# Local attention scores as three split products, their low parts made on VectorE

## The chip, the cores and the metric

The kernel runs on one core of one Trainium2 chip. The metric is the device time of one execution in microseconds. The engines are TensorE (PE), VectorE (DVE), ScalarE (ACT), GpSimd (POOL) and SyncE (SP), each with its own instruction stream, coupled by semaphores.

## The reference

Two layers over x (512 tokens, 1024 channels). Each layer forms u = RMSNorm(x), one combined input projection, three branches (a gated short convolution, gated linear attention, local attention), a gated sum of the branches, the output projection, and then an MLP. The change lies in the local attention: 8 query heads, 2 key heads, 64 channels a head, blocks of 128 queries against their own and the previous block of 128 keys.

```python
q = rms_norm(q.reshape(Bsz, S, SWA_HEADS, SWA_HEAD_DIM).astype(f32), qn_w)
k = rms_norm(k.reshape(Bsz, S, SWA_KV_HEADS, SWA_HEAD_DIM).astype(f32), kn_w)
q = rope_partial(q, cos, sin) * SWA_HEAD_DIM ** -0.5
k = rope_partial(k, cos, sin)
s = jnp.einsum('bnqkgd,bnckd->bkgnqc', qb, kw)
s = jnp.where(mask, s, -jnp.inf)
m = jnp.maximum(jnp.max(s, axis=-1, keepdims=True), sink)
p = jnp.exp(s - m)
denom = jnp.sum(p, axis=-1, keepdims=True) + jnp.exp(sink - m)
o = jnp.einsum('bkgnqc,bnckd->bkgnqd', p, vw) / denom
```

## The kernel before

All large products are split products. A float32 matrix is held as a high part of type float32r and a low part (value minus high part), and PE adds three products: high by high, high by low, low by high. ACT makes the high part of each weight unit, DVE the low part (L1229, `split_low`), and PE waits for `lo_done` of the unit. The small products of the branches, the attention scores among them, are plain float32.

Every engine runs down a list of words written out by hand: PE_ORDER, ACT_ORDER, DVE_ORDER for the projection and branch stage. A word with a plus is a weight split (`+gr2` is the split of the weight unit gr2); the others are steps. `gr0.0` on PE is one token tile of a projection unit. The words that matter here, in the stage of local attention:

- KD and QT0 to QT3: PE transposes the key and four pairs of query heads into a PSUM bank (L738). ACT copies the bank to SBUF (L1027, tiles `swa_k` and `swa_q`), frees the bank and adds one to `qT_ready`.
- ATT0, ATT1: products and masking of the linear attention (PE L754, DVE L1471).
- SC0 to SC7: the scores, on PE L810, in banks a and b for even and odd heads. SC0 to SC3 are the four query blocks of the first half of the heads, SC4 to SC7 those of the second. SC0 and SC4 have 128 keys, the others 256. SC waits for `qT_ready` of its half. On DVE the step SC masks the scores and takes the row maxima (L1520 to L1534); on ACT it is the exponential.
- SM: DVE forms the reciprocal sum (L1538, L1540), ACT scales the probabilities.
- PT: PE transposes the probabilities (L820), DVE copies them under a mask to `probs_keys` (L1546) and adds one to `probs_T_ready`.
- PV: PE multiplies the probabilities with the values (L828), after `probs_T_ready`.
- KV0, KV1: states of the linear attention (PE L767, DVE L1477 and L1482).

The four banks go round: a step may fill a bank when the step four fills before it has been read. QT2 takes the bank of QT0, SC0 the banks of ATT1, QT3 that of QT1, KV0 those of SC0b and QT3.

The score call of one pair of heads and one row half is

```python
last = nc.tensor.matmul(
    both[odd][:, j * 2 * P + first:(j + 1) * 2 * P],
    sq[r:r + SWA_DIM, 2 * half + j, n * P:(n + 1) * P],
    kd[r:r + SWA_DIM, (n - 1) * P + first:(n + 1) * P], start=True, stop=True)
```

with j and odd from 0 to 1, so four calls a block and 64 in the program.

Of the kernel before, what the change touches and what calls it, by code (L numbers as in the profile page):

```python
# [9 lines left out]
D_MODEL, SEQ, DEPTH = 1024, 512, 2  # L10
P = 128
# [3 lines left out]
SWA_HEADS, SWA_KV, SWA_DIM = 8, 2, 64  # L15
# [5 lines left out]
             sq=512, sk=128, sv=128, gates=N_BRANCH * D_MODEL)  # L21
# [72 lines left out]


DVE_ORDER = """+gk1 UT0 UT1 UT2 UT3 RN +kva0 NROW gk0 +kva1 +kva2 gk1 +kva3 +sq0 +sq1 kva0 kva1 kva2 kva3 +sq2 AT +sq3 +gv0 ZA ZB
sq0 sq1 sq2 sq3 +gv1 +gv2 X0 +gv3 QS +gr0 QM +gr1 X1 QR ATT0 +gr2 ATT1 +gr3 SC0 +cx0 SM0 SC1 KV0 SM1 PT0 +cx1 KV1 PV0 PT1 +cx2
gr0 SC2 gr1 gr2 SC3 gr3 +cx3 SM2 GO0 SM3 cx0 GO1 OS PT2 YG0 cx1 YG1 +cc0 +cc1 cx2 +cc2 PV1 PV2 cx3 +cc3 PT3 SC4 cc0 ct0 SM4
SC5 +cb0 YT0 +cb1 cc1 PV3 SM5 cc2 +cb2 YT1 PT4 cc3 SC6 +cb3 YT2 PV4 SM6 cv0 PT5 +gate0 YT3 ct1 SC7 cl0 ct2 SM7 PT6 PV5 cv1 cv2
+gate1 +gate2 cl1 PT7 ct3 +gate3 PV6 cv3 cl2 +br0 cl3 gate0 PV7 gate1 +br1 gate2 +br2 gate3""".split()  # L100
# [133 lines left out]
def hybrid_trunk(nc, x, x_cols, positions, params, w_in, gla_wa2, w_branch, w_o, w_up, w_down, norms, consts, gmask, out):  # L234
    f32, f32r, i32 = mybir.dt.float32, mybir.dt.float32r, mybir.dt.int32
    ALU, ACT, AX = mybir.AluOpType, mybir.ActivationFunctionType, mybir.AxisListType
    ctx = ExitStack()
    with ctx:
# [3 lines left out]
        def at(name, tile, shape, dt=f32, extra=0):  # L242
            return nc.alloc_sbuf_tensor_at(name, [P] + shape, dt, offset=BASE + tile * TILE + extra)
# [43 lines left out]
        attm = at("gla_att", 76, [GLA_HEADS, TT, P])  # L287
        sm = [at(f"probs{i}", 80 + 2 * i, [4, P]) for i in range(2)]
        gt = at("gate_tanh", 80, [4, SEQ])
        sq = at("swa_q", 84, [4, SEQ])  # L290
        kd = at("swa_k", 88, [SEQ])
        vd = at("swa_v", 90, [TT, SWA_KV, SWA_DIM])
        pT = at("probs_keys", 91, [2, 4, P])
        th = [at(f"gla_gate_tanh{i}", (93, 98)[i], [SEQ]) for i in range(2)]
# [68 lines left out]
        def sem(name):  # L363
# [21 lines left out]
         conv_val, conv_hi, yconv_ready, pv_hi, yswa_ready, scores_ready, exps_ready, den_ready,  # L385
         probs_ready, probs_T_ready, gate_scaled, gate_ready, mixed_done, mx_hi, mx_ready, x_upd,
         x_summed, u_hi, u_ready, hid_val, hid_hi, hid_ready, sums_val, sums_hi, sums_ready, diff_val, diff_hi,
         diff_ready, ws_val, ws_hi, ws_ready, wg_ready, g_full, x_left_added, x_right_added, folded, fold_scaled, x_top_folded, x_low_folded, x_first_added, angle_ready, sines_ready, first_full, first_hi, first_lo, probs_T_zero) = map(sem, """
         par_free hi_done lo_done unit_done tile_done bank_full ready0 rs_ready a_ready ga_ready
         z_biased softplus_ready b_ready gla_exps gla_qk kva_read sq_sq sq_summed v_ready gr_tanh rg_ready  # L390
         kendT_ready att_ready states_ready yo_sq yo_summed ytok_ready gla_hi ygla_ready q_roped qT_ready
         conv_val conv_hi yconv_ready pv_hi yswa_ready scores_ready exps_ready den_ready
         probs_ready probs_T_ready gate_scaled gate_ready mixed_done mx_hi mx_ready x_upd
         x_summed u_hi u_ready hid_val hid_hi hid_ready sums_val sums_hi sums_ready diff_val diff_hi
         diff_ready ws_val ws_hi ws_ready wg_ready g_full x_left_added x_right_added folded fold_scaled x_top_folded x_low_folded x_first_added angle_ready sines_ready first_full first_hi first_lo probs_T_zero""".split())

        UNIT_CREDIT = SPLIT

# [176 lines left out]
        def _(pe):  # L575
# [127 lines left out]
            for l in range(DEPTH):  # L703
                for step in PE_ORDER if l else PE_FIRST + PE_ORDER[PE_ORDER.index("kva0"):]:
                    word, pieces = pieces_of(step)
                    kind, i = step_of(word)
# [66 lines left out]
                    elif kind == "GO":  # L773
                        both = [open_bank(l, word + half) for half in "ab"]
                        pe.wait_ge(att_ready, l * 4 + 4)
                        pe.wait_ge(states_ready, l * 2 + 2)
                        for t in (2 * i, 2 * i + 1):
                            for pair in range(2):
                                at_o = slice((t % 2 * 2 + pair) * P, (t % 2 * 2 + pair + 1) * P)
                                for odd in range(2):  # L780
                                    h = 2 * pair + odd
                                    nc.tensor.matmul(both[odd][:, at_o], attm[:, h, t, :], vt[:, t, h * P:(h + 1) * P],  # L782
                                                     start=t % 2 + pair == 0, stop=False)
                        for c in range(4 * i, 4 * i + 4):
                            to = slice(GLA_CHUNK * (c % 2), GLA_CHUNK * (c % 2 + 1))
                            for pair in range(2 if c else 0):
                                at_o = slice((c // 2 % 2 * 2 + pair) * P, (c // 2 % 2 * 2 + pair + 1) * P)
                                for odd in range(2):
                                    r = GLA_DK * odd
                                    last = nc.tensor.matmul(both[odd][to, at_o],  # L790
                                                            gq[r:r + GLA_DK, pair, c * GLA_CHUNK:(c + 1) * GLA_CHUNK],
                                                            S[r:r + GLA_DK, pair, c - 1, :], start=False,
                                                            stop=c % 4 >= 2 and pair == 1)
                                    if c % 4 == 3 and pair == 1:
                                        last.then_inc(bank_full, 1)
                    elif kind == "YT":
                        b = open_bank(l, word)
                        pe.wait_ge(ytok_ready, l * 2 + 2)
                        for t in range(TT):
                            last = nc.tensor.transpose(b[:, t * P:(t + 1) * P], yo[t // 2][:, t % 2, i, :], ident)  # L800
                        last.then_inc(bank_full, 1)
                    elif kind == "SC":
                        half, n = i // TT, i % TT
                        pe.wait_ge(qT_ready, l * 5 + 3 + 2 * half)
                        both = [open_bank(l, word + part) for part in "ab"]
                        first = 0 if n else P
                        for j in range(2):
                            for odd in range(2):
                                r = SWA_DIM * odd
                                last = nc.tensor.matmul(  # L810
                                    both[odd][:, j * 2 * P + first:(j + 1) * 2 * P],
                                    sq[r:r + SWA_DIM, 2 * half + j, n * P:(n + 1) * P],
                                    kd[r:r + SWA_DIM, (n - 1) * P + first:(n + 1) * P], start=True, stop=True)
                                if j == 1:
                                    last.then_inc(bank_full, 1)
                    elif kind == "PT":
                        pe.wait_ge(probs_ready, l * 8 + i + 1)
                        b = open_bank(l, word)
                        for h in range(4):
                            last = nc.tensor.transpose(b[:, h * P:(h + 1) * P], sm[i % 2][:, h, :], ident)  # L820
                        last.then_inc(bank_full, 1)
                    elif kind == "PV":
                        half, n = i // TT, i % TT
                        b = open_bank(l, word)

                        def weighted(kv, cur):
                            r = SWA_DIM * kv
                            return nc.tensor.matmul(b[r:r + SWA_DIM, 2 * kv * P:(2 * kv + 2) * P], vd[:, n - 1 + cur, kv, :],  # L828
                                                    pT[:, cur, 2 * kv:2 * kv + 2, :].rearrange("p h c -> p (h c)"),
                                                    start=cur == 0 or n == 0, stop=cur == 1)  # L830
                        pe.wait_ge(probs_T_ready, l * 8 + i + 1)
                        if n:
                            for kv in range(SWA_KV):
                                weighted(kv, 0)
                        for kv in range(SWA_KV):
                            last = weighted(kv, 1)
                        last.then_inc(bank_full, 1)
# [36 lines left out]
        def _(act):  # L874
# [6 lines left out]
            def filled(l, name):  # L881

                f = FILL[l, name]
                act.wait_ge(bank_full, f + 1)
                return bank[f % 4], bank_free[f % 4]
# [68 lines left out]
            for l in range(DEPTH):  # L954
                for word in ACT_ORDER:
# [67 lines left out]
                        nc.scalar.activation(kendT[:, i].rearrange("p t n -> p (t n)"), b[:], ACT.Copy).then_inc(free, 1)  # L1023
                        nc.scalar.drain().then_inc(kendT_ready, 1)
                    elif kind in ("KD", "QT"):
                        b, free = filled(l, word)
                        nc.scalar.activation(kd[:] if kind == "KD" else sq[:, i, :], b[:], ACT.Copy).then_inc(free, 1)  # L1027
                        nc.scalar.drain().then_inc(qT_ready, 1)
                    elif kind == "GO":
                        if i:  # L1030
                            act.wait_ge(yo_summed, l * 4 + 2)
# [177 lines left out]
        def _(dve):  # L1209
# [8 lines left out]
            def filled(l, name):  # L1218

                f = FILL[l, name]  # L1220
                dve.wait_ge(bank_full, f + 1)
                return bank[f % 4], bank_free[f % 4]
# [107 lines left out]
            for l in range(DEPTH):  # L1330
                for word in DVE_ORDER if l else DVE_FIRST + DVE_ORDER[DVE_ORDER.index("+kva3") + 1:]:
# [173 lines left out]
                    elif kind == "YT":  # L1505
# [2 lines left out]
                        V.scalar_tensor_tensor(out=yl[:, 4 + i, :], in0=b[:], scalar=par[:, PC["on"]:PC["on"] + 1],  # L1508
                                               in1=yh[:, 4 + i, :].bitcast(f32), op0=ALU.mult, op1=ALU.subtract).then_inc(free, 1)
                        V.drain().then_inc(ygla_ready, 1)  # L1510
                    elif kind == "SC":
                        buf = i % 2
                        if i >= 2:
# [297 lines left out]
```

## Time and profile before

| | before |
|---|---|
| median of 3 runs | 1562.13 us (1561.9 to 1562.47) |
| the profiled execution | 1561.48 us |
| its span, first to last instruction | 1559.7 us |
| PE busy | 1548.6 us (99%) |
| DVE busy | 1051.2 us (67%) |
| ACT busy | 753.5 us (48%) |
| POOL busy | 113.0 us (7%) |
| granted TensorE clock over the span | 1.000 |

The span is one execution taken by the profiler. Busy is the time in which an engine ran at least one instruction. The recorded matmuls of PE overlap, since they are pipelined, so the distance between their starts tells their cost, not their duration. A row of a timeline puts like instructions together; a count behind x is their number, and its start is that of the first one.

### The profile page before, as it was taken

The numbers are of one execution on the slowest core, as the hardware profiler recorded it, in microseconds if no ns is written. First come the engines' busy times: TensorE is split into PE (matmuls) and PEld (weight loads), VectorE is DVE, ScalarE is ACT, GpSimd is POOL, SyncE is SP. The second block draws the span as 40 slices with busy tenths as digits, with TensorE's granted clock in tenths as the row PEclk, the third lists the DMA queues.
The fourth block names the chain that finished last, engine by engine and source line by source line (L and its number), as shares of the span: only waits on it lengthen the run. The fifth ranks groups of instructions, "written<-read, shape, count | busy, mean of one in ns | idle before, by whom it ended". The sixth has DMA issues, their size and how long they took to land.

```text
span 1559.7 us, 21296 instructions
## 1 busy us (share of the span) xinstructions
PE 1548.6 (99%) x7440; PEld 1266.4 (81%) x7440; DVE 1051.2 (67%) x1529; ACT 753.5 (48%) x1147; POOL 113.0 (7%) x97
## 2 busy tenths in 40 slices
PE   8999999999999999999999999999999999999999
PEld 7877778888878888888888777788888788888887
DVE  5677774555777657586857787755457676665778
ACT  5656532223556463546546465332236564636363
POOL 0000000000211010111200000000002111101011
PEclk9999999999999999999999999999999999999999
DMA  6321314532686655647533212155317856666555
GB/s 228 116 83 57 107 54 149 176 114 75 133 213 160 181 133 151 170 109 206 89 101 102 82 55 82 55 175 176 108 54 149 242 122 186 139 174 137 137 133 122
DMA packets 133722, 204.16 MB, mean 131 GB/s; under 512 B 6704, under 2 KB 83056, under 8 KB 133616
## 3 DMA queue, kind: packets, MB, share of 16 engines
q1 hardware_dynamic: 107600, 153.30, 29.5%
q0 software_dynamic: 25296, 48.76, 18.7%
q8 instruction: 60, 0.98, 0.3%
q10 hardware_dynamic: 720, 0.74, 0.1%
q14 instruction: 46, 0.38, 0.1%
HBM read 170.80 MB, written 2.10 MB: 111 GB/s over the span
## 4 chain that ended last, share of the span: by engine, by line
PE 87%; DVE 8%; issue 2%; DVEq 1%; DMA 1%; ACT 1%; ACTq 0%; POOL 0%; POOLq 0%
PE acc L609 19%; PE acc L611 19%; PE acc L610 19%; PE acc L672 5%; PE acc L673 5%; PE acc L674 5%; DVE wl_rows L1229 3%; PE acc L631 3%; PE acc L633 3%; PE acc L632 3%; PE bank L810 1%; PE bank L828 1%; DMA x_tokens<-product_sums 0%; DVE mixed_s_lo L1580 0%; PE bank L782 0%
## 5 line engine op out<-in xcount | busy, mean ns | idle before, releaser
L609 PE MATMUL acc<-uh,wh 128*128 128x512 f32 x1152 | 452.9, 393 | 2.6 <-DVEq L1250 2.5
L611 PE MATMUL acc<-uh,wl 128*128 128x512 f32 x1152 | 448.6, 389 | 0.0
L610 PE MATMUL acc<-ul,wh 128*128 128x512 f32 x1152 | 448.5, 389 | 0.0
L609 PEld LDWEIGHTS acc<-uh,wh 128*128 128x128 f32 x1152 | 216.3, 188 | 54.8 <-issue 5.0
L611 PEld LDWEIGHTS acc<-uh,wl 128*128 128x128 f32 x1152 | 216.3, 188 | 45.4
L610 PEld LDWEIGHTS acc<-ul,wh 128*128 128x128 f32 x1152 | 216.4, 188 | 43.5
L1229 DVE TENSOR_TENSOR wl<-raw,wh 128x1024 fp32r<-128x1024 f32 x142 | 174.0, 1225 | 103.4 <-ACT wh L903 91.2
L903 ACT ACTIVATE wh<-raw 128x1024 fp32r<-128x1024 f32 x142 | 150.6, 1061 | 138.6 <-PE acc L611 86.3
L903 ACT ACTIVATE wh_rows<-raw_down 128x1024 fp32r<-128x1024 f32 x136 | 144.3, 1061 | 109.7 <-PE acc L674 89.0
L1229 DVE TENSOR_TENSOR wl_rows<-raw_down,wh_rows 128x1024 fp32r<-128x1024 f32 x136 | 166.6, 1225 | 23.1 <-ACT wh_rows L903 11.2
L1073 ACT ACTIVATE gate_tanh<-gate_tanh 128x512 f32<-128x512 f32 x40 | 25.3, 633 | 164.4 <-DVEq L1260 164.4
L1259 DVE TENSOR_TENSOR gate_tanh<-acc,rsqrt_rows 128x512 f32<-128x512 f32 x48 | 33.2, 691 | 97.6 <-PE acc L611 96.5
L1122 ACT ACTIVATE hidden<-acc 128x512 f32<-128x512 f32 x64 | 38.3, 599 | 122.1 <-PE acc L611 120.3
L631 PE MATMUL acc<-wh_rows,uh 128*128 128x512 f32 (+1 forms) x256 | 95.9, 375 | 0.0
L633 PE MATMUL acc<-wl_rows,uh 128*128 128x512 f32 (+1 forms) x256 | 93.4, 365 | 0.0
L632 PE MATMUL acc<-wh_rows,ul 128*128 128x512 f32 (+1 forms) x256 | 93.3, 364 | 0.0
L1159 POOL DMA_DIRECT2D raw_down<-raw_down x20 | 24.2, 1209 | 809.1 <-DMA raw_down<-in_w_o_dram 568.9
L672 PE MATMUL acc<-wh_rows,hidden_hi 128*128 128x512 f32 x192 | 75.1, 391 | 0.0
L609 PE MATMUL acc<-yh,wh 128*128 128x512 f32 x192 | 74.8, 389 | 0.0
L674 PE MATMUL acc<-wl_rows,hidden_hi 128*128 128x512 f32 x192 | 74.7, 389 | 0.0
L673 PE MATMUL acc<-wh_rows,hidden_lo 128*128 128x512 f32 x192 | 74.7, 389 | 0.0
L611 PE MATMUL acc<-yh,wl 128*128 128x512 f32 x192 | 74.7, 389 | 0.0
(268 smaller groups left out, 2435.1 us busy)
## 6 DMA issues: line engine op xcount, KB each, us to landing
raw<-in_w_in_dram SPq DMA_DIRECT2D x39, 1024.0 KB, 5.2
raw<-in_w_up_dram SPq DMA_DIRECT2D x32, 1024.0 KB, 5.9
raw_down<-in_w_down_dram SPq DMA_DIRECT2D x32, 1024.0 KB, 8.9
raw_down<-raw_down POOLq DMA_DIRECT2D x44, 512.0 KB, 5.1
raw_down<-in_w_down_dram POOLq DMA_DIRECT2D x32, 512.0 KB, 6.2
raw_branch<-in_w_in_dram SPq DMA_DIRECT2D x12, 1024.0 KB, 5.0
raw_branch<-in_w_branch_dram SPq DMA_DIRECT2D x12, 1024.0 KB, 5.1
raw_down<-in_w_o_dram SPq DMA_DIRECT2D x8, 1024.0 KB, 8.4
```

The source lines that it names most:

```text
L609: nc.tensor.matmul(a[:], wh[slot][:, k, :], right_h, start=at_k == 0, stop=False)
L610: nc.tensor.matmul(a[:], wh[slot][:, k, :], right_l, start=False, stop=False)
L611: last = nc.tensor.matmul(a[:], wl[slot][:, k, :], right_h, start=False, stop=at_k == n - 1)
L631: nc.tensor.matmul(to, left_h[:, k, s], h[:, row, 0:cols], start=k == 0, stop=False)
L632: nc.tensor.matmul(to, left_l[:, k, s], h[:, row, 0:cols], start=False, stop=False)
L633: last = nc.tensor.matmul(to, left_h[:, k, s], lo[:, row, 0:cols], start=False, stop=k == KT - 1)
L672: nc.tensor.matmul(to[:], left[0], h[:, row, :], start=k == 0, stop=False)
L673: nc.tensor.matmul(to[:], left[1], h[:, row, :], start=False, stop=False)
L674: last = nc.tensor.matmul(to[:], left[0], lo[:, row, :], start=False, stop=k == BK - 1)
L903: nc.scalar.activation(split_view(True, u, l), raw_view(u), ACT.Copy).then_inc(hi_done, 1)
L1122: nc.scalar.activation(hid[:, k, :], a[:], ACT.Relu).then_inc(free, 1)
L1229: V.tensor_tensor(split_view(False, u, l), raw_view(u), split_view(True, u, l).bitcast(f32), ALU.subtract).then_inc(lo_done, 1)
```

## The change

ACT writes the copies of key and queries as float32r (`k_hi`, `q_hi`) and no longer frees the bank. DVE gets the steps KD and QT0 to QT3: it waits for ACT's copy (`qT_hi`), subtracts it from the bank, writes `k_lo` or `q_lo`, frees the bank and adds one to `qT_ready`. PE makes each score as three products into the same bank region, so a block has 12 calls in place of 4. In DVE_ORDER the splits gr2, gr3, cx0 and cx1 change places with other steps. Apart from rounding the result is the same.

```diff
 DVE_ORDER
-sq0 sq1 sq2 sq3 +gv1 +gv2 X0 +gv3 QS +gr0 QM +gr1 X1 QR ATT0 +gr2 ATT1 +gr3 SC0 +cx0 SM0 SC1 KV0 SM1 PT0 +cx1 KV1 PV0 PT1 +cx2
+sq0 sq1 sq2 sq3 +gv1 +gv2 X0 +gv3 QS +gr0 QM +gr1 X1 QR ATT0 KD QT0 ATT1 QT1 QT2 +gr2 SC0 QT3 +gr3 SM0 SC1 KV0 SM1 +cx0 PT0 KV1 PV0 +cx1 PT1 +cx2
...
-        sq = at("swa_q", 84, [4, SEQ])
-        kd = at("swa_k", 88, [SEQ])
+        q_hi = at("swa_q_hi", 84, [4, SEQ], f32r)
+        q_lo = [at(f"swa_q_lo{i}", (100, 101, 81, 83)[i], [SEQ], f32r) for i in range(4)]
+        k_hi, k_lo = at("swa_k_hi", 88, [SEQ], f32r), at("swa_k_lo", 89, [SEQ], f32r)
...
                         for j in range(2):
-                            for odd in range(2):
-                                r = SWA_DIM * odd
-                                last = nc.tensor.matmul(
-                                    both[odd][:, j * 2 * P + first:(j + 1) * 2 * P],
-                                    sq[r:r + SWA_DIM, 2 * half + j, n * P:(n + 1) * P],
-                                    kd[r:r + SWA_DIM, (n - 1) * P + first:(n + 1) * P], start=True, stop=True)
-                                if j == 1:
-                                    last.then_inc(bank_full, 1)
+                            for term, (q, k) in enumerate(((q_hi[:, 2 * half + j], k_hi), (q_hi[:, 2 * half + j], k_lo),
+                                                           (q_lo[2 * half + j], k_hi))):
+                                for odd in range(2):
+                                    r = slice(SWA_DIM * odd, SWA_DIM * (odd + 1))
+                                    last = nc.tensor.matmul(both[odd][:, j * 2 * P + first:(j + 1) * 2 * P], q[r, queries],
+                                                            k[r, keys], start=term == 0, stop=term == 2)
+                                    if j == 1 and term == 2:
+                                        last.then_inc(bank_full, 1)
...
                     elif kind in ("KD", "QT"):
-                        b, free = filled(l, word)
-                        nc.scalar.activation(kd[:] if kind == "KD" else sq[:, i, :], b[:], ACT.Copy).then_inc(free, 1)
-                        nc.scalar.drain().then_inc(qT_ready, 1)
+                        b, _ = filled(l, word)
+                        nc.scalar.activation(k_hi[:] if kind == "KD" else q_hi[:, i, :], b[:], ACT.Copy).then_inc(qT_hi, 1)
...
+                    elif kind in ("KD", "QT"):
+                        b, free = filled(l, word)
+                        dve.wait_ge(qT_hi, l * 5 + (1 if kind == "KD" else i + 2))
+                        low, high = (k_lo[:], k_hi[:]) if kind == "KD" else (q_lo[i][:], q_hi[:, i, :])
+                        V.tensor_tensor(low, b[:], high.bitcast(f32), ALU.subtract).then_inc(free, 1)
+                        V.drain().then_inc(qT_ready, 1)
```

On DVE, from the mask copy of ATT0 to the start of SC0, there stood before (`wl_rows` with a number is the low part of a weight unit, gr2 and gr3 here; `gla_att` is ATT):

```order
L1471 COPY_PREDICATED gla_att<-masks,bank 128x512 x2
L1229 TENSOR_TENSOR wl_rows_72<-raw_branch_55,wh_rows_68 128x1024
L1471 COPY_PREDICATED gla_att<-masks,bank 128x512 x2
L1229 TENSOR_TENSOR wl_rows_73<-raw_branch_55,wh_rows_69 128x1024
L1525 TENSOR_TENSOR probs_103<-bank,consts 128x256 x2
```

and stands now, on to the split of gr3:

```order
L1472 COPY_PREDICATED gla_att<-masks,bank 128x512 x2
L1516 TENSOR_TENSOR swa_k_lo<-bank,swa_k_hi 128x512
L1516 TENSOR_TENSOR swa_q_lo_107<-bank,swa_q_hi 128x512
L1472 COPY_PREDICATED gla_att<-masks,bank 128x512 x2
L1516 TENSOR_TENSOR swa_q_lo_108<-bank,swa_q_hi 128x512
L1516 TENSOR_TENSOR swa_q_lo_109<-bank,swa_q_hi 128x512
L1230 TENSOR_TENSOR wl_rows_72<-raw_branch_55,wh_rows_68 128x1024
L1532 TENSOR_TENSOR probs_103<-bank,consts 128x256 x2
...
L1516 TENSOR_TENSOR swa_q_lo_110<-bank,swa_q_hi 128x512
L1230 TENSOR_TENSOR wl_rows_73<-raw_branch_55,wh_rows_69 128x1024
```

Two low parts stand ahead of ATT1's mask copy, two behind it, and one behind SC0; the split of gr2 moved behind four of them, that of gr3 behind SC0.

On DVE, between SM1 (the last `small` rows) and PT1, the order was before (`wl_63` is the low part of cx1, `probs_keys` is PT, `yl` is PV):

```order
L1540 RECIPROCAL small<-small 128x4
L1546 COPY_PREDICATED probs_keys<-masks,bank 128x512
L1229 TENSOR_TENSOR wl_63<-raw_52,wh_59 128x1024
L1477 COPY gla_states<-bank 128x128
L1482 SCALAR_TENSOR_TENSOR gla_states<-gla_states,gla_exp_b,bank 128x128 x6
L1557 TENSOR_TENSOR yl<-bank,yh 64x2x128 x2
L1546 COPY_PREDICATED probs_keys<-masks,bank 128x512 x2
```

and is now (`wl_62` is the low part of cx0):

```order
L1547 RECIPROCAL small<-small 128x4
L1230 TENSOR_TENSOR wl_62<-raw_52,wh_58 128x1024
L1553 COPY_PREDICATED probs_keys<-masks,bank 128x512
L1478 COPY gla_states<-bank 128x128
L1483 SCALAR_TENSOR_TENSOR gla_states<-gla_states,gla_exp_b,bank 128x128 x6
L1564 TENSOR_TENSOR yl<-bank,yh 64x2x128 x2
L1230 TENSOR_TENSOR wl_63<-raw_52,wh_59 128x1024
L1553 COPY_PREDICATED probs_keys<-masks,bank 128x512 x2
```

The split of cx0, which stood behind SC0, is now directly ahead of PT0, and that of cx1 moved from behind PT0 to behind PV0.

On PE the block SC0 was one row of four calls:

```order
L632 MATMUL acc<-wh_rows_66,ul 128x512
L633 MATMUL acc<-wl_rows_70,uh 128x512
L810 MATMUL bank<-swa_k,swa_q 128x128 x4
L738 MATMUL bank<-consts,swa_qk_tokens 128x128 x4
L631 MATMUL acc<-wh_rows_66,uh 128x512
```

and is now:

```order
L634 MATMUL acc<-wl_rows_70,uh 128x512
L814 MATMUL bank<-swa_k_hi,swa_q_hi 128x128 x2
L814 MATMUL bank<-swa_k_lo,swa_q_hi 128x128 x2
L814 MATMUL bank<-swa_k_hi,swa_q_lo_107 128x128 x2
L814 MATMUL bank<-swa_k_hi,swa_q_hi 128x128 x2
L814 MATMUL bank<-swa_k_lo,swa_q_hi 128x128 x2
L814 MATMUL bank<-swa_k_hi,swa_q_lo_108 128x128 x2
L739 MATMUL bank<-consts,swa_qk_tokens 128x128 x4
```

Its neighbours are the same, and the place of every score block in PE's list is unchanged.

## Rows read from the trace of the kernel before

**Rows 1.** The page, busy time, share of the span and instructions of TensorE.

```profile
PE 1548.6 (99%) x7440; PEld 1266.4 (81%) x7440; DVE 1051.2 (67%) x1529; ACT 753.5 (48%) x1147; POOL 113.0 (7%) x97
```

**Rows 2.** Waits of TensorE in the whole span: total, times, longest.

```profile
PE acc L609 <- DVEq L1250: 2.5, 1, 2.5
...
PE bank L689 <- DVEq L1634: 0.2, 1, 0.2
```

**Rows 3.** Line L810: durations in ns, first and last start, shapes.

```profile
L810 PE MATMUL bank<-swa_k,swa_q x128: 272/376/480, 99.9 to 970.6; 64*128 64x256 f32 x96, 64*128 64x128 f32 x32
```

**Rows 4.** The chain, TensorE, 94 to 125 us: start, length, piece.

```profile
99.92 0.65 PE bank L810 x8
...
105.28 1.06 PE bank L810 x8
```

**Rows 5.** The timeline, TensorE, inside two score blocks: start, duration, instructions.

```profile
105.53 0.60 PE L810 MATMUL bank<-swa_k,swa_q 64*128 64x256 f32 x4
...
105.75 0.60 PE L810 MATMUL bank<-swa_k,swa_q 64*128 64x256 f32 x4
...
100.07 0.50 PE L810 MATMUL bank<-swa_k,swa_q 64*128 64x128 f32 x6
...
100.18 0.39 PE L810 MATMUL bank<-swa_k,swa_q 64*128 64x128 f32 x4
```

**Rows 6.** The timeline, TensorE, split products with 272 columns.

```profile
44.01 0.29 PE L633 MATMUL acc<-wl_rows,uh 128*128 128x272 f32 x1
44.14 0.29 PE L631 MATMUL acc<-wh_rows,uh 128*128 128x272 f32 x1
```

**Rows 7.** The timeline, VectorE, 93 to 114 us, idle before in brackets.

```profile
93.10 1.61 DVE L1471 COPY_PREDICATED gla_att<-masks,bank 128x512 f32<-128x512 int32 x2 [0.23 <-issue]
94.90 1.23 DVE L1229 TENSOR_TENSOR wl_rows<-raw_branch,wh_rows 128x1024 fp32r<-128x1024 f32 x1 [0.19 <-issue]
96.23 1.61 DVE L1471 COPY_PREDICATED gla_att<-masks,bank 128x512 f32<-128x512 int32 x2
...
100.60 0.75 DVE L1525 TENSOR_TENSOR probs<-bank,consts 128x256 f32<-128x256 f32 x2 [1.35 <-PE bank L810]
...
102.53 0.15 DVE L1534 TENSOR_TENSOR small<-params,small 128x4 f32<-128x4 f32 x1
...
105.56 0.16 DVE L1538 TENSOR_TENSOR small<-small 128x4 f32<-128x4 f32 x1 [0.60 <-ACT small L1047]
...
106.38 0.42 DVE L1520 COPY probs<-bank 128x256 f32<-128x256 f32 x1 [0.40 <-PE bank L810]
...
113.55 0.74 DVE L1546 COPY_PREDICATED probs_keys<-masks,bank 128x512 f32<-128x512 int32 x1 [0.23 <-issue]
```

**Rows 8.** The page, the multiplication by a row out of an accumulator.

```profile
L1259 DVE TENSOR_TENSOR gate_tanh<-acc,rsqrt_rows 128x512 f32<-128x512 f32 x48 | 33.2, 691 | 97.6 <-PE acc L611 96.5
```

**Rows 9.** The timeline, ScalarE, 96 to 119 us.

```profile
96.50 0.60 ACT L1027 ACTIVATE swa_q<-bank 128x512 f32<-128x512 f32 x1 [0.15 <-issue]
...
105.34 0.19 ACT L1047 ACTIVATE small<-small 128x4 f32<-128x4 f32 x1
...
118.20 1.06 ACT L903 ACTIVATE wh<-raw 128x1024 fp32r<-128x1024 f32 x1 [2.26 <-PE acc L633]
```

**Rows 10.** The timeline, TensorE, 99 to 115 us.

```profile
99.86 0.71 PE L810 MATMUL bank<-swa_k,swa_q 64*128 64x128 f32 x8
...
113.43 1.09 PE L767 MATMUL bank<-gla_v_tokens,gla_k_end_tokens 64*64 64x128 f32 x28
114.48 0.65 PE L828 MATMUL bank<-probs_keys,swa_v 128*64 128x256 f32 x4
```

**Rows 11.** The chain, TensorE, second layer, 870 to 892 us.

```profile
874.37 0.65 PE bank L810 x8
...
888.97 0.62 PE bank L828 x4
```

**Rows 12.** The page, DMA issues: count, size, median us to landing.

```profile
raw<-in_w_in_dram SPq DMA_DIRECT2D x39, 1024.0 KB, 5.2
```

More of the change, by code:

```diff
@@ L387, in hybrid_trunk @@
          x_summed, u_hi, u_ready, hid_val, hid_hi, hid_ready, sums_val, sums_hi, sums_ready, diff_val, diff_hi,
-         diff_ready, ws_val, ws_hi, ws_ready, wg_ready, g_full, x_left_added, x_right_added, folded, fold_scaled, x_top_folded, x_low_folded, x_first_added, angle_ready, sines_ready, first_full, first_hi, first_lo, probs_T_zero) = map(sem, """
+         diff_ready, ws_val, ws_hi, ws_ready, wg_ready, g_full, x_left_added, x_right_added, folded, fold_scaled, x_top_folded, x_low_folded, x_first_added, angle_ready, sines_ready, first_full, first_hi, first_lo, probs_T_zero, qT_hi) = map(sem, """
          par_free hi_done lo_done unit_done tile_done bank_full ready0 rs_ready a_ready ga_ready
@@ L394, in hybrid_trunk @@
          x_summed u_hi u_ready hid_val hid_hi hid_ready sums_val sums_hi sums_ready diff_val diff_hi
-         diff_ready ws_val ws_hi ws_ready wg_ready g_full x_left_added x_right_added folded fold_scaled x_top_folded x_low_folded x_first_added angle_ready sines_ready first_full first_hi first_lo probs_T_zero""".split())
+         diff_ready ws_val ws_hi ws_ready wg_ready g_full x_left_added x_right_added folded fold_scaled x_top_folded x_low_folded x_first_added angle_ready sines_ready first_full first_hi first_lo probs_T_zero qT_hi""".split())
         UNIT_CREDIT = SPLIT
@@ L806, in _ @@
                         first = 0 if n else P
+                        queries, keys = slice(n * P, (n + 1) * P), slice((n - 1) * P + first, (n + 1) * P)
                         for j in range(2):
-                            for odd in range(2):
-                                r = SWA_DIM * odd
-                                last = nc.tensor.matmul(
-                                    both[odd][:, j * 2 * P + first:(j + 1) * 2 * P],
-                                    sq[r:r + SWA_DIM, 2 * half + j, n * P:(n + 1) * P],
-                                    kd[r:r + SWA_DIM, (n - 1) * P + first:(n + 1) * P], start=True, stop=True)
-                                if j == 1:
-                                    last.then_inc(bank_full, 1)
+                            for term, (q, k) in enumerate(((q_hi[:, 2 * half + j], k_hi), (q_hi[:, 2 * half + j], k_lo),
[6 more added lines that the diff above has]
+                                        last.then_inc(bank_full, 1)
                     elif kind == "PT":
```

## Prediction

> **What bounds the kernel now.** I read the page's busy times first. TensorE (PE) is busy for 99% of the span [rows 1], so the question is whether the change shortens PE's work or makes PE wait. The waits of PE came next: in the whole execution it has six, the longest 2.5 us, and none is at a score block or at a product of probabilities and values [rows 2]. PE runs as one unbroken chain, and a microsecond added to it or taken from it anywhere is a microsecond of the result. Then I read the changed line, L810, by shape: 128 recorded matmuls, two for each of the 64 calls, so a float32 product runs as two passes [rows 3]. 96 of them have 256 moving columns, 32 have 128. Per layer there are eight score blocks: six wide (SC1 to SC3 and SC5 to SC7), two narrow (SC0 and SC4). Last I followed DVE and ACT from the first score block to PV0, because the change puts DVE between ACT and PE there.
>
> **The score blocks on PE.** The chain gives 1.06 us to a wide block and 0.65 to a narrow one [rows 4]. Inside a block the odd and even heads use different row halves and start together, in pairs; the starts of neighbouring pairs (105.53 and 105.75 in the wide block, 100.07 and 100.18 in the narrow one [rows 5]) are about 0.215 and 0.11 us apart. Four pair steps leave a fixed part of 1.06 - 4 x 0.215 = 0.20 us, and 0.65 - 0.44 = 0.21 in the narrow block, for the change of tile shape before and behind.
>
> After the change a block has six pair steps of one pass each, two head pairs times three terms. No row shows such a step. The nearest is a split product with 272 columns, which starts every 0.125 us [rows 6]; the lower bound is the narrow step of today, 0.11, which has the same 128 columns to load. I take 0.12. A wide block becomes 6 x 0.12 + 0.20 = 0.92 us, a gain of 0.14 (0.20 at a step of 0.11, 0.11 at 0.125). A narrow block is bounded by its load and becomes 6 x 0.11 + 0.21 = 0.87, a loss of 0.22. Could a split product with few columns be slower? If its step cost what both float32 passes of a pair cost, 0.22, a narrow block would be 1.5 us, a loss of 0.9. I take 0.11 and keep that end. If only this counted, the kernel would change by -12 x 0.14 + 4 x 0.22 = -0.8 us.
>
> **The wait at SC0.** SC0 now needs the low parts of key, QT0 and QT1, all from DVE. DVE's ATT0 starts at 93.10, takes 1.61 and ends at 94.71 [rows 7]. For a low part (128x512 out of PSUM) I use the 0.691 us of L1259 [rows 8], with 0.18 between steps, the gap in front of the weight split at 94.90. The low part of the key is then done at 95.6. QT0's needs its high part, and ACT starts that at 96.50 and takes 0.60 [rows 9]: DVE idles until 97.16 and is done at 97.85. ATT1, which started at 96.23, starts at 98.03 and ends at 99.64. QT1's low part ends at 100.51. From DVE to PE I take 0.19: PT0's copy starts at 113.55, ends at 114.29, and PV0 starts at 114.48 [rows 7, 10]. SC0 starts at 100.70 in place of 99.86 [rows 10]: PE waits 0.84 us.
>
> **The wait at PV0.** This is the larger one. PV0 needs PT0's copy, and 114.48 is where PE arrives anyway: KV1 starts at 113.43 and occupies PE for 1.02 to 1.09. So there is no slack in front of PV0. DVE from 100.51 on:
>
> QT2 low 0.87; the gr2 split 1.42 (1.23 and a gap); SC0, from 100.60 to the end of its last operation (102.53 + 0.15), with a gap 2.2; QT3 low 0.87; the gr3 split 1.42; SM0 0.6; a gap of 0.2 [rows 7]. That is 7.6 us, and SC1 starts at 108.1 in place of 106.38. ACT's exponentials for SM0 do not decide it: today they end (105.34 + 0.19 [rows 9]) 2.85 us after SC0 on DVE, with a weight split ahead of them, so at the latest at 105.0 + 2.85 = 107.9, 0.4 behind where I put SM0. From SC1's start to PT0's start DVE works through 7.17 us without waiting for anyone (106.38 to 113.55), and cx0's split now stands inside that stretch, another 1.3 to 1.4. PT0 starts at 116.6, ends at 117.3, and PE starts PV0 at 117.5: 3.0 us late. On its own, PE would be late by 0.84 + 0.22 (SC0) - 0.14 (SC1) = 0.9. The other 2.1 are a wait at PV0, and up to there the length of the PE blocks no longer matters; even the dear narrow block (0.9) is absorbed.
>
> As a cross-check: five low parts with gaps are 4.35 us of new DVE work and the idling for QT0 is 1.6, together 5.9; DVE's idle of today goes (1.35, 0.60 and 0.40 [rows 7], and 1.04 between SC0's end at 102.68 and cx0's split, which starts at 105.56 - 0.60 - 1.23 = 103.73), and 5.9 less part of 3.4 leaves about 3.
>
> Queued behind DVE's PT0 are KV1, PV0, cx1's split, PT1, cx2's split and SC2. None of them gains a step, so they are late by no more than PT0, and PE, which consumes them, is late by the same 3.0: no third wait. The second layer is the same: SC0 at 874.37 and PV0 at 888.97 in the chain are 14.60 apart [rows 11], in the first layer 99.86 and 114.48 are 14.62 [rows 10]. So 2 x 3.0 = 6.0.
>
> **What is hidden.** The weight splits themselves: gr3's split frees a raw buffer 8 us later (at 105.0 + 0.87 + 1.42 = 107.3, today at 100.60 - 1.35 = 99.25), its transfer lands 5.2 us after issue [rows 12], and ACT's first use of it is the split at 118.20, released by PE [rows 9]. Over 5 us of cover remain. ACT has the same activations and two drains fewer.
>
> **The sum.** 6.0 up to PV0 in both layers; behind it ten wide blocks gain 10 x 0.14 = 1.4 and two narrow ones lose 0.4: +5.0 us. The profiled execution took 1561.48 us (its span 1559.7), 0.65 under the median of 1562.13. It becomes 1566.5, and the median **1567.1**.
>
> **Where a page disagrees.** The trace has weight loads on PE hidden although a block returns to the same row half with every second matmul: a narrow float32 pair streams and still steps at 0.11. The Trainium skill, TensorE: Matmul & The Clock Gate, section "The mechanism", has loads overlapping running matmuls only when their row groups differ, or when they go to the background buffer; by the first half alone, each load (estimate from the same page: columns / 1.2 GHz, 107 ns) would stand in the open, steps would be about 0.21, and the result about 1574. The measured 0.11 speaks for the background buffer, so this has 0.03 of the third case below.
>
> **Rivals.**
> 1. DVE catches up, and PV0 does not wait. It would if low parts were cheaper or DVE's idle absorbed them; then only PE's own sum (-0.8) and the waits at SC0 (0 to 1.7) are left: 1561.3 to 1563.0, not slower. For it: DVE idles 3.4 us between 99.25 and 106.38 [rows 7]. Against it: 1.6 of new waiting for ACT, and a split moved ahead of PT0. It decides if DVE's chain is 2.1 us shorter per layer than I have it. With partial catching up (a delay at PV0 under 2 us per layer) the total stays below +3. Together 0.24.
> 2. The forecast: PV0 late by 2 to 3.5 us in each layer, narrow blocks cheap or dear (dear adds 2 x 0.65 = 1.3): 1565.3 to 1569. 0.66.
> 3. Split products of different row halves do not pair, or their loads are not hidden: steps of 0.21 to 0.24. A wide block is 1.46 to 1.64 (+0.40 to +0.58), a narrow one about 1.5 (+0.85). Up to PV0 the wait absorbs it; behind it, ten wide blocks add 4.0 to 5.8 and two narrow ones 1.7, so 6.0 + 5.7 to 7.5: 1574 to 1576. For it: the trace has no split product on 64 rows. Against it: L767's 28 passes of 128 columns, on 64 rows too, fit into 1.09 us [rows 10], 0.04 each, so such passes do run side by side. 0.08.
> 4. Clearly faster. All blocks at the lower bound give 12 x 0.20 = 2.4 less 0.9, so this needs something that I don't see. 0.02.
>
> A measurement of this kernel can tell about 0.2% (3.1 us) from no change. Faster 0.02; same 0.24; slower 0.74. The range is 1562.5 to 1571: it takes in most of the first case, all of the second, and leaves the third out.
>
> **What would show it.** A wait of PE at the score line for DVE's low part, about 0.8 us, twice; a wait at the probabilities-times-values line for the copy of PT0, about 2 us, twice; wide blocks of 0.92 and narrow ones of 0.87; ATT1 at 98.0 and PT0 at 116.6 on DVE. If PE shows no wait at PV0, my DVE chain is wrong; if the pair steps are near 0.24, the pairing is.

## The result, and the profile after

The changed kernel takes 1569.51 us (median of 6 runs, 1568.2 to 1571.61) against 1562.16 us (6 runs, 1561.71 to 1562.47) for the kernel before. The ratio is 1.0049, with a 95% interval of 1.0038 to 1.0059: slower by about 7.4 us. The prediction was 1567.1 us, in a range of 1562.5 to 1571.0. The profiled execution took 1569.49 us and its span is 1567.7 us, 8.0 more than before; the forecast had +5.0. Of the eleven executions of the run e7_late below, two took 3155 and 7986 us, with no cause on record; its median leaves them out.

Line numbers moved: the scores are L814, the product of probabilities and values (PV) is L830, the low parts L1516, the copies of the probabilities (PT) L1553, the states of the linear attention (KV) L768 on PE and L1483 on DVE, the weight split on DVE L1230.

TensorE's waits in the changed kernel, answering to [rows 2]:

```profile
PE bank L830 <- DVEq L1556: 5.0, 2, 2.5
PE bank L702 <- DVEq L1217: 2.2, 1, 2.2
PE acc L610 <- DVEq L1251: 1.8, 1, 1.8
PE bank L814 <- DVEq L1517: 1.5, 2, 0.7
```

The first and the fourth are new, and they are the two that were forecast: PV0 waits for the copy of PT0 (2.5 us per layer, forecast 2.1), SC0 for QT1's low part (0.75, forecast 0.84). The largest other new wait is 0.2 us per layer ahead of a KV product (L768), put down to issue.

The score blocks in the chain (start, length, piece), answering to [rows 4]:

```profile
100.81 0.89 PE bank L814 x12
...
106.40 0.91 PE bank L814 x12
```

and the start of SC0 with the wait ahead of it, and the inside of SC1, in TensorE's timeline, answering to [rows 5]:

```profile
100.81 0.33 PE L814 MATMUL bank<-swa_k_hi,swa_q_hi 64*128 64x128 f32 x2 [0.75 <-DVEq L1517]
...
106.33 0.39 PE L814 MATMUL bank<-swa_k_hi,swa_q_hi 64*128 64x256 f32 x2
106.55 0.28 PE L814 MATMUL bank<-swa_k_lo,swa_q_hi 64*128 64x256 f32 x2
106.67 0.28 PE L814 MATMUL bank<-swa_k_hi,swa_q_lo 64*128 64x256 f32 x2
106.78 0.28 PE L814 MATMUL bank<-swa_k_hi,swa_q_hi 64*128 64x256 f32 x2
```

A wide block takes 0.91 us (forecast 0.92), a narrow one 0.89 in the chain (0.87). The pairs start 0.11 to 0.12 us apart, apart from the first one of a block, which follows a product of another tile shape (0.22 in the wide block, 0.16 in the narrow one). So the split products are what they were taken for, and the wide blocks did get shorter, 1.06 to 0.91.

VectorE's timeline in the changed kernel, answering to [rows 7] (idle time before the row in brackets):

```profile
93.24 1.61 DVE L1472 COPY_PREDICATED gla_att<-masks,bank 128x512 f32<-128x512 int32 x2 [0.23 <-issue]
95.11 0.69 DVE L1516 TENSOR_TENSOR swa_k_lo<-bank,swa_k_hi 128x512 fp32r<-128x512 f32 x1 [0.26 <-issue]
97.26 0.69 DVE L1516 TENSOR_TENSOR swa_q_lo<-bank,swa_q_hi 128x512 fp32r<-128x512 f32 x1 [1.46 <-ACT swa_q_hi L1029]
98.14 1.61 DVE L1472 COPY_PREDICATED gla_att<-masks,bank 128x512 f32<-128x512 int32 x2 [0.19 <-issue]
100.02 0.69 DVE L1516 TENSOR_TENSOR swa_q_lo<-bank,swa_q_hi 128x512 fp32r<-128x512 f32 x1 [0.26 <-issue]
...
108.35 0.42 DVE L1527 COPY probs<-bank 128x256 f32<-128x256 f32 x1 [0.17 <-PE bank L768]
...
115.36 0.16 DVE L1545 TENSOR_TENSOR small<-small 128x4 f32<-128x4 f32 x1 [0.83 <-issue]
115.60 0.18 DVE L1547 RECIPROCAL small<-small 128x4 f32<-128x4 f32 x1
115.95 1.23 DVE L1230 TENSOR_TENSOR wl<-raw,wh 128x1024 fp32r<-128x1024 f32 x1 [0.17 <-issue]
117.33 0.73 DVE L1553 COPY_PREDICATED probs_keys<-masks,bank 128x512 f32<-128x512 int32 x1 [0.16 <-issue]
```

ATT1 starts at 98.14 (forecast 98.03), SC1 at 108.35 (108.1), PT0 at 117.33 (116.6). DVE never caught up.

What the forecast did not have stands in the windows view of TensorE (stretch, length, busy time and matmuls, granted clock, DMA share and GB/s):

```profile
110.00:114.00 4.00, 4.00 (x21) 1.00 0.58 202
114.00:118.00 4.00, 1.55 (x31) 1.00 0.01 2
118.00:122.00 4.00, 3.75 (x11) 0.57 0.00 0
122.00:126.00 4.00, 4.00 (x29) 1.00 0.23 44
...
892.00:896.00 4.00, 1.93 (x32) 1.00 0.01 2
896.00:900.00 4.00, 3.37 (x10) 0.57 0.00 0
```

After each of the two waits at PV0 the granted clock is at its lower level, 1.2 GHz, for about 3.5 us (118.25 to 121.77 in the chain below), and full, 2.4 GHz, again behind that (0.57 is a mean over 4 us). In the chain the products behind PV0 show it:

```profile
118.25 1.12 PE bank L830 x4
119.37 0.73 PE acc L632
120.10 0.43 PE acc L633
...
121.77 0.23 PE acc L634
```

PV0 takes 1.12 us where it took 0.65 [rows 10], and a split product of 512 columns 0.43 in place of 0.23. Put beside the trace of before, QT3's transposition behind SC0 starts 1.12 us late, PV0 3.77, and the product at 121.8 us 5.28: 1.51 us are lost at the low clock in the first layer, and in the second 1.45 (7.70 late at PV0, 9.15 behind it).

### The profile page after: what moved, and what is told of

It reads as the page before. It is cut to its first block, busy times and chain, and to the rows that moved or that the text cites. A ratio compares the mean times of both kernels' runs of the same rounds, so it can differ in the third digit from the quotient of the medians.

```text
span 1567.7 us, 21454 instructions
## 1 busy us (share of the span) xinstructions
PE 1550.9 (99%) x7504; PEld 1270.0 (81%) x7504; DVE 1058.5 (68%) x1539; ACT 753.9 (48%) x1147; POOL 113.0 (7%) x97
## 4 chain that ended last, share of the span: by engine, by line
PE 84%; DVE 10%; DVEq 2%; issue 1%; ACT 1%; DMA 1%; SPq 0%; ACTq 0%
PE acc L610 19%; PE acc L611 19%; PE acc L612 19%; PE acc L675 6%; PE acc L673 6%; PE acc L674 6%; DVE wl_rows L1230 3%; PE acc L632 2%; PE acc L633 2%; PE acc L634 2%; PE bank L830 1%; PE bank L814 1%; DMA raw<-in_w_in_dram 1%; DVE x_tokens L1623 1%; PE bank L690 0%
## 5 line engine op out<-in xcount | busy, mean ns | idle before, releaser
L1230 DVE TENSOR_TENSOR wl<-raw,wh 128x1024 fp32r<-128x1024 f32 x142 | 174.0, 1225 | 103.4 <-ACT wh L905 90.9
L1230 DVE TENSOR_TENSOR wl_rows<-raw_down,wh_rows 128x1024 fp32r<-128x1024 f32 x136 | 166.6, 1225 | 21.7 <-ACT wh_rows L905 9.7
```

The lines of the kernel that those rows point to most:

```text
L1230: V.tensor_tensor(split_view(False, u, l), raw_view(u), split_view(True, u, l).bitcast(f32), ALU.subtract).then_inc(lo_done, 1)
```

## The experiments

The theory after reading this trace: the loss is one chain on DVE, whose end (PT0's copy) holds PV0, and a second cost that this wait brings along, the low clock. The rivals: the split products cost something themselves; the low clock is their doing and not the wait's; the moved weight splits are free. The lines of an order show only the words around the change.

**Only the order of the splits (e1_order).** On the kernel before:

```diff
-QR ATT0 +gr2 ATT1 +gr3 SC0 +cx0 SM0 SC1 KV0 SM1 PT0 +cx1 KV1 PV0 PT1 +cx2
+QR ATT0 ATT1 +gr2 SC0 +gr3 SM0 SC1 KV0 SM1 +cx0 PT0 KV1 PV0 +cx1 PT1 +cx2
```

> The kernel before with only the order of DVE's weight splits changed: gr2 behind ATT1, gr3 behind SC0, cx0 ahead of PT0, cx1 behind PV0, as in the changed kernel; the scores stay plain float32 and there are no low parts. Theory A (DVE's chain sets PV0, so cx0's split ahead of PT0 costs its length): PT0 starts about 1.3 us later on DVE than the 113.55 of before, PE waits about 1.3 us at PV0 in each layer, +2.6, so about 1564.8 us as long as the granted clock stays full; if a wait of this length also lets the clock fall to half, up to 3 more, 1567.8. Rival B (the order is free, DVE's idle time absorbs the moved splits): no wait at PV0, 1562.2. It also says how much of the loss is the low parts': A leaves them about 1.2 us of lateness at PV0 per layer plus SC0's wait.

1564.59 us against 1561.92 (ratio 1.0017, 1.0007 to 1.0026). TensorE's waits:

```profile
PE bank L828 <- DVEq L1549: 2.5, 2, 1.3
```

and the windows view around the first one:

```profile
114.00:118.00 4.00, 2.73 (x29) 1.00 0.01 2
118.00:122.00 4.00, 4.00 (x25) 1.00 0.00 0
```

Theory A, with the clock at full at both waits (the 0.999 over this profile's span is not lost there). A third of the loss comes with the order alone, without a single low part.

**Only PE's blocks (e2_products).** On the changed kernel, with DVE's order of before and ACT freeing the bank. The low parts are left out, so its scores lack them:

```diff
...
-                            for term, (q, k) in enumerate(((q_hi[:, 2 * half + j], k_hi), (q_hi[:, 2 * half + j], k_lo),
-                                                           (q_lo[2 * half + j], k_hi))):
+                            for term, (q, k) in enumerate(((q_hi[:, 2 * half + j], k_hi), (q_hi[:, 2 * half + j], k_hi),
+                                                           (q_hi[:, 2 * half + j], k_hi))):
...
```

> The changed kernel's PE blocks alone: 12 calls a score block, but all three terms are high part by high part, so the scores are three times the high product and no low part is made (this part of the computation is left out); ACT frees the bank as before and DVE has its old order. Theory A (the products are a small gain, the loss is all DVE's chain and what follows from it): twelve wide blocks at 0.91 in place of 1.06, four narrow ones at 0.81 to 0.87 in place of 0.65, -1.8 + 0.8 = about -1.0, so 1561.2 us, no wait at SC0 or PV0 and a full clock throughout. Rival B (the split products themselves cost, by tile changes or by the clock): 1563 or more, with a granted clock under 1 in these stretches.

1560.33 us (1559.93 to 1560.64) against 1561.92 (0.9991, 0.9981 to 1.0): 1.6 us less in the medians, with no wait at L814 or L830 and a clock of 1.0. The products are not the cost; by the medians they are a small gain, though the interval of the ratio reaches 1. In this trace the wide blocks each bring the next product of PE 0.12 to 0.18 us forward against the trace before.

**PE kept busy during the wait (e3_fill).** On the changed kernel:

```diff
+if i == 0:
+    for _ in range(10):
+        nc.tensor.matmul(b[:], uh[:, 0, 0:P], uh[:, 0, :], start=True, stop=True)
 pe.wait_ge(probs_T_ready, l * 8 + i + 1)
```

> The changed kernel with ten extra matmuls (128x512, into the bank that PV0 is about to overwrite) on PE ahead of PV0's wait for the copied probabilities, some 2.3 us that fill the wait of 2.5 us. They add nothing to the result. Theory A (behind the wait the granted clock falls to half for 3.4 us, because PE stood idle, and that costs about 1.5 us per layer): the clock stays full and the time is about 3.0 us under the changed kernel's, 1566.5 us. Rival B (the clock falls for another reason, such as the stretch of small tiles ahead, or the half clock costs nothing): 1569.5 us, or a little more if the extra work overruns the wait.

1566.42 us (1566.0 to 1566.58), 3.1 under the changed kernel (2.9 when each is taken against the runs of before beside it), although PV0 still cannot start before DVE's copy (117.75, in a profile whose stage began 0.4 us earlier). The extra matmuls and what follows, from TensorE's timeline:

```profile
115.26 2.56 PE L835 MATMUL bank<-uh 128*128 128x512 f32 x10
117.75 0.65 PE L830 MATMUL bank<-probs_keys,swa_v 128*64 128x256 f32 x4
118.33 0.50 PE L632 MATMUL acc<-wh_rows,uh 128*128 128x512 f32 x1
```

and the windows view behind them:

```profile
118.00:122.00 4.00, 4.00 (x20) 1.00 0.00 0
...
892.00:896.00 4.00, 4.00 (x22) 1.00 0.03 6
896.00:900.00 4.00, 4.00 (x22) 1.00 0.00 0
```

PV0 takes 0.65 us again, and the clock stays full in both layers. Work that adds nothing to the result gives back the 3.0 us (1.51 + 1.45) that the low clock cost. That is theory A, to 0.1 us in the median.

**A long wait in the kernel before (e10_wait).** The order of e1_order with one more split ahead of PT0, so no split products in the scores and no low parts of key and queries:

```diff
-SM1 +cx0 PT0 KV1 PV0 +cx1 PT1 +cx2
+SM1 +cx0 +cx1 PT0 KV1 PV0 PT1 +cx2
```

> The kernel before (plain float32 scores, no low parts) with two weight splits, cx0 and cx1, ahead of PT0 on DVE, gr2 behind ATT1, gr3 behind SC0, so that PE waits at PV0 for about 2.6 us per layer without anything else of the change. Theory A (the fall of the granted clock comes from PE's idle time of this length, whatever kernel it stands in): PV0 2.6 late, 1562.0 + 5.2 = 1567.2 with a full clock, and about 1.6 more for each layer in which it falls, so most executions at 1568.8 or 1570.4 and the clock column under 1. Rival B (the split products are what lets the clock fall, by drawing more or by their small tiles): 1567.2 in all executions, with a clock of 1.

1571.49 us (1570.32 to 1572.06), granted clock over the span 0.996 to 0.998 in all five runs. The wait, and the windows view of its profile:

```profile
PE bank L828 <- DVEq L1549: 5.3, 2, 2.7
```

```profile
114.00:117.00 3.00, 0.49 (x17) 1.00 0.00 0
117.00:120.00 3.00, 2.85 (x8) 0.50 0.94 290
...
896.00:899.00 3.00, 3.00 (x9) 0.50 1.01 322
899.00:902.00 3.00, 3.00 (x8) 0.50 0.08 24
902.00:905.00 3.00, 3.00 (x19) 0.98 0.00 0
```

The clock falls here too, so it goes with PE's idle time and not with the split products of the scores: rival B is out. The cost was above my figure: in the second layer the low clock lasts some 6 us and costs 2.9 in place of the 1.6 I had put, which about accounts for the step from 1570.4 to the 1571.5 measured.

**The cx0 split behind PT0 (e4_cx0).** On the changed kernel:

```diff
-SM1 +cx0 PT0 KV1 PV0 +cx1 PT1 +cx2
+SM1 PT0 +cx0 KV1 PV0 +cx1 PT1 +cx2
```

> The changed kernel with the split of cx0 behind PT0 on DVE, as in the kernel before; all else as changed. Theory A (DVE's chain up to PT0 sets PV0's start): PT0 1.3 us earlier, so the wait at PV0 falls from 2.5 to about 1.2 us per layer, -2.6: 1566.9 us with the clock still falling behind a wait of 1.2 us, or 1563.9 us if so short a wait no longer lets it fall. Rival B (cx0's split comes too late for PE's cx0 tiles, or ACT's release of the next unit is late): a new wait of PE at the projection behind PV0 takes the place of the old one, 1569.5 us.

1566.3 us (1565.99 to 1566.44) against 1561.92. Neither expectation holds as put. TensorE's waits:

```profile
PE bank L830 <- DVEq L1556: 2.4, 2, 1.2
...
PE bank L783 <- DVE probs L1529: 2.1, 2, 1.1
```

PV0's wait fell to 1.2 us and the clock is full, as A has it, which would be 1563.9. But a wait of 1.1 us per layer is new, at the products of the linear attention (L783): PE may fill that bank only when SC2 on DVE has read it, and cx0, cx1 and cx2 are now all split between PT0 and SC2. It is rival B's kind of event in another place. The time came back 12 us further on.

**QT0's high part earlier (e5_actq).** ACT's order in the changed kernel:

```diff
-KD +gr3 gv3 QT0 QT1 QT2 QT3
+KD QT0 +gr3 gv3 QT1 QT2 QT3
```

> The changed kernel with one step of ACT moved: the high part of QT0 directly behind that of the key, ahead of the gr3 split and gv3. DVE's order is as changed. Theory A (DVE's idle 1.46 us for QT0's high part is one link of the chain that ends at PV0): DVE is 1.3 us earlier from QT0's low part on, SC0's wait (0.75 per layer) is gone, PV0 starts 1.3 earlier, so its wait is 2.5 - 1.3 + 0.75 = 1.95 us; 1569.5 - 2.6 = 1566.9 if the clock still falls to half behind it, 1563.9 if it stays full. Rival B (ACT is the tighter one, and gv3 or the gr3 split, now later, holds up a transposition or a product): a new wait on ACT, 1569 or more.

The median is 1565.64 us against 1561.99 (1.0026, 1.0016 to 1.0035), but its ten runs stand on three levels, and the granted clock over the span goes with them: 1563.79 (clock 1.000, the profiled one); 1565.27 to 1566.07 in six (0.999); 1567.12 to 1567.51 in three (0.997 and 0.998). SC0's wait is gone, and PV0's is

```profile
PE bank L830 <- DVEq L1556: 4.7, 2, 2.4
```

2.4 us, longer than the 1.95 I had, because PE now arrives 1.2 us earlier and PT0 only 1.4. In the profiled execution the clock stays full behind both waits (windows view):

```profile
118.00:122.00 4.00, 4.00 (x20) 1.00 0.00 0
892.00:896.00 4.00, 3.57 (x17) 1.00 0.00 0
```

The levels are 1.6 to 1.8 us apart, close to the 1.5 us that one fall of the clock cost above, and lie about where A put its ends (1563.9 without, 1566.9 with both). So behind waits of 2.4 us the clock stayed full in the traced execution; that it fell in one layer in six of the others and in both in three is read from their times and clocks and not traced. The waits of 2.5 and 2.7 us above did it in both layers of their profiles. The other executions of the changed kernel vary too: one took 1568.2 us at a clock of 0.999, one 1571.61 at 0.996.

**Both at once (e6_both).** The two edits together.

> QT0's high part earlier on ACT and cx0's split behind PT0 on DVE, both at once. Theory A (two waits in one DVE chain, PV0 and, 10 us on, the first product of linear attention that needs the bank that SC2 on DVE frees, as the run with cx0's split behind PT0 alone showed with 1.1 us per layer): PV0's wait falls under 1 us, but three splits between PT0 and SC2 keep the second one, so the delay per layer is that of DVE's SC2, 1.3 less than the 3.4 us at that place in the run with only the split moved: 1566.3 - 2.6 = 1563.7 us. Rival B (PV0 was the only place that mattered): 1561.0 to 1561.7 us.

1563.98 us (1563.73 to 1564.58; expected 1563.7), ratio 1.0013. PV0 and L783 wait 1.1 us each per layer, the clock is full. A holds, but for PV0's wait, which it had under 1 us; PV0 is not the only place.

**Later splits (e7_late, e8_gr3, e9_cx1).** On top of e6_both (the line with the minus), DVE's order became, in e7_late, e8_gr3 and e9_cx1 (the three lines with a plus):

```diff
-QT3 +gr3 SM0 SC1 KV0 SM1 PT0 +cx0 KV1 PV0 +cx1 PT1 +cx2 gr0 SC2 gr1 gr2 SC3 gr3 +cx3
+QT3 +gr3 SM0 SC1 KV0 SM1 PT0 KV1 PV0 +cx0 PT1 gr0 SC2 +cx1 gr1 gr2 SC3 +cx2 gr3 +cx3
+QT3 SM0 SC1 KV0 SM1 PT0 +gr3 KV1 PV0 +cx0 PT1 gr0 SC2 +cx1 gr1 gr2 SC3 +cx2 gr3 +cx3
+QT3 SM0 SC1 KV0 SM1 PT0 +gr3 KV1 PV0 +cx0 PT1 gr0 SC2 gr1 gr2 SC3 +cx1 gr3 +cx2 +cx3
```

> As the run before in this list, and on DVE the splits behind PV0 moved as well: cx0 behind PV0, cx1 behind SC2, cx2 behind SC3, since PE needs these units only at and behind the projection tiles that follow. Theory A: the second wait goes too, what is left is PV0 late by 0.5 to 1.0 us per layer, on top of the 1560.3 us of the run with only the PE blocks: 1561.3 to 1562.3 us. Rival B (a later split lets its raw buffer go later, and a transfer or an ACT split comes late): a wait of ACT for a raw unit and of PE at the projection, 1564 or more.

1561.48 us against 1561.99 (0.9998, 0.9989 to 1.0008). PV0 still waits 1.1 per layer, L783 no longer.

> As the run before, and the gr3 split behind PT0 as well, so DVE has before PT0 no more than the low parts and gr2 as additions or moves. Theory A (with enough weight splits moved behind the steps that PE waits for, the low parts fit into DVE's idle time): no wait at SC0, PV0 or behind, the granted clock full, and the time is that of the PE blocks alone, 1560.3 to 1560.8 us, about 1.3 under the kernel before. Rival B (gr3's raw buffer is freed 8 us later still than in the changed kernel, its 5.2 us transfer lands after ACT wants it for cx2 at 118 to 120 us): ACT and then PE wait, 1562 or more.

1561.5 us (0.9998, 0.9989 to 1.0007), not the 1560.3 to 1560.8 expected. PV0's wait is down to 0.3 us, but PE waits three times at L783, 1.6 us in all, in a profile of the slowest execution (1562.65). In the first layer cx1's split now makes SC3 late on DVE, and PE's second pair of linear-attention products waits for SC3's bank (in TensorE's timeline the wait is put down to issue; the bank's last reader, L1529, ends at 133.2):

```profile
133.29 2.02 PE L783 MATMUL bank<-gla_v_tokens,gla_att 128*128 128x128 f32 x16 [0.45 <-issue]
```

In the second layer the first pair waits 0.66 us and the second 0.49. So the 0.7 in the next text belongs to the first pair.

> As the run with the gr3 split behind PT0, and the cx1 split one step later still, behind SC3 on DVE. In that run PE's second pair of linear-attention products waited 0.45 us in the first layer and 0.7 in the second for the bank that SC3 on DVE frees, with cx1's split standing ahead of it. Theory A (it is the last wait of the DVE chain): that wait goes, the time falls by about 1.2 us to 1560.3 us, within 0.3 of the run with only the PE blocks (1560.3), and clearly under the kernel before. Rival B (cx1's low part or the next ACT split is late): a wait of PE at a projection tile, 1561.5 or more.

1560.8 us (1560.09 to 1561.34) against 1561.94 (1561.41 to 1563.72), ratio 0.9992, interval 0.9983 to 1.0001: 0.5 above the 1560.3 expected. The waits at L783 are gone. TensorE's waits at the changed places are down to

```profile
PE bank L830 <- DVEq L1556: 1.1, 4, 0.3
```

This is the changed kernel with the same arithmetic and all its low parts, from 7.4 us over the kernel before to 1.1 under it by the order of ACT's and DVE's words alone. Its slowest run is faster than the fastest of before in this comparison, but the interval of the ratio just includes 1, so "not slower, perhaps 0.1% faster" is all that is shown.

## Why the prediction was right, and where it was short

**The split products on PE: right.** Steps of 0.11 to 0.12 us, blocks of 0.91 and 0.89, pairs in parallel, loads hidden. The third rival (steps of 0.21 to 0.24) is refuted by the rows above, and e2_products shows the gain by itself: -1.6 us in the medians, where the step-by-step sum had -0.8. The argument for the pairing was thinner than the prediction has it: the products of L767 that run side by side have tiles of 64 x 64 [rows 10], not the 64 x 128 of the scores.

**The wait at SC0: right**, 0.75 for 0.84, and by the named cause: DVE idles 1.46 us for QT0's high part. e5_actq moved that high part and the wait went.

**The wait at PV0: the mechanism right, the size short by 0.6 us per layer.** Relative to the start of the stage (0.14 us late already) PV0 is 3.63 us late, forecast 3.0. 0.1 is in the gaps behind the low parts (0.26 in place of 0.18). 0.5 is a gap of 0.83 us in front of SM1, where before there were 0.34. KV0 ends with drains, steps that wait until DVE has finished and then free a bank; the second of them comes late, as the chain of the changed kernel shows:

```profile
114.53 0.03 DVEq L1485
114.56 0.44 issue
115.00 0.14 DVEq L1486
```

The long gap stands in every kernel here that has low parts (0.70 to 0.83) and in none of e1_order, e2_products and e10_wait (0.34). Why is open; no run takes it apart. e1_order and e4_cx0 confirm the term of cx0's split from both sides (PE 1.31 later with it, 1.26 earlier without).

**"No third wait": right for the changed kernel, but for a reason that I had not seen.** PE is so late behind PV0 that DVE has its later steps done in time. As soon as PV0 was relieved (e4_cx0), a third wait of 1.1 us appeared at L783, and with more relief (e8_gr3) a fourth. The splits that I costed at nothing behind PV0 were covered by the very wait in front of them. ("Two drains fewer" on ACT is a miscount: the change removes one from each of the five steps KD and QT0 to QT3, ten in the program. Nothing in the sum used it.)

**Missing: the clock.** The forecast took the granted clock of before, 1.000, as given. After each wait at PV0 it fell to 1.2 GHz for some 3.5 us: 1.51 + 1.45 = 3.0 us. This is the step that failed, "PE, which consumes them, is late by the same 3.0": PE is late by the wait and then slower for a while. e3_fill gives the 3.0 back without removing the wait, e10_wait makes the fall in a kernel without the change. The Trainium skill, TensorE: Matmul & The Clock Gate, section "Part 1: The HAM clock gate", says that the clock depends on how busy PE has recently been, and calls its warm-up "run-variable". The traces agree with the first (full in e3_fill, low behind the same wait left empty), and the clock behind a wait varies from one execution to the next here too (e5_actq). My forecast priced a wait of PE at its own length alone. It had put that wait at 2.1 us; no run here has one between 1.3 and 2.4 us at PV0, so whether a wait of 2.1 would have let the clock fall is not shown.

**The sum.** By the traces: PV0 2 x 3.63, the clock 3.0, the blocks behind PV0 -0.6 per layer (forecast -1.0 in all), and -0.8 at places outside the score blocks (at the opening of the second layer and of the last stage) that I have not traced; with 0.14 at the start this is 8.4 at the last products and 8.0 in the span. The medians differ by 7.35. The forecast's +5.0 is 3.0 short through the clock and 1.2 through PV0, and 1.2 over elsewhere. So it was in part luck that the number held: the median lies 0.5 us above the 1565.3 to 1569 of the forecast's own case, in a stretch of the range for which the forecast names no mechanism.

## What to carry to other kernels

When a step is put on an engine in front of one that never waits, cost the whole in-order queue up to the next hand-over, and then ask what that queue is late for once the first wait is relieved: here relieving PV0 moved the wait to the products 12 us on (e4_cx0, e6_both), and relieving those moved it to the next pair (e8_gr3). Work without a near deadline (the weight splits, whose products come some 10 us and more behind them in the changed kernel) belongs behind the steps that feed the busy engine; that, and one step of ACT made earlier, turned +7.4 us into -1.1.

A forecast wait of TensorE as long as those here (2.4 us and more) is not paid with its own length: read the granted clock behind waits of that length in the traces at hand, and put a second term (1.5 us each here, once 2.9), with a chance, into the sum.

## What the runs showed of the hardware

- The granted clock fell to 1.2 GHz after idle times of PE of 2.5 us (the changed kernel) and 2.7 us (e10_wait), in both layers, in a kernel that is otherwise 99% busy. It stayed there for some 3.5 us in the changed kernel and up to some 6 us in e10_wait. Waits of 1.2 and 1.3 us (e4_cx0, e1_order) did not show it in their profiles. The kernel before has a wait of 2.5 us of its own [rows 2], at the very start, and there the granted clock stays at 1.00, as the stretch with it shows (the windows view of the kernel before, TensorE):

```profile
8.00:12.00 4.00, 2.09 (x8) 1.00 1.07 383
```

  In e5_actq the wait of 2.4 us did not do it in the traced execution, and by times and clocks did it in others. So the length of the wait does not decide alone; what does is open.
- The spread of a kernel's runs goes with it: 3.4 us for the changed kernel and 3.7 for e5_actq, 0.6 for e3_fill and 0.45 for e4_cx0.
- Split products of float32r on the two 64-row halves run in pairs, with starts 0.11 to 0.12 us apart for 128 as for 256 columns, where a float32 call of 256 columns stepped at 0.215. With 128 columns three split products are therefore dearer than one float32 product (narrow block 0.65 to 0.89), with 256 they are cheaper (wide block 1.06 to 0.91).
